# Modulation product of an adaLN transformer block, with its operands exchanged

## What is computed

```
def modulate(x, shift, scale):
    return rms_norm(x) * (1.0 + scale) + shift
def adaln(cond, w, b):
    return jnp.split(jax.nn.silu(cond) @ w + b, 6, axis=-1)
```

## Time and profile before

| | |
|---|---|
| median of 3 runs | 3432.3 us |
| the profiled execution | 3440.02 us |
| its span, first to last instruction | 3438.2 us |
| TensorE (PE) busy | 3122.3 us, 91% |
| TensorE weight loads (PEld) busy | 2324.8 us, 68% |
| VectorE (DVE) busy | 1697.6 us, 49% |
| ScalarE (ACT) busy | 963.3 us, 28% |
| mean granted TensorE clock | 0.941 of 2.4 GHz |

### The profile page before, as it was taken

One profiled execution on the slowest core, in us unless ns is written; L12 is line 12 of the kernel. 1 busy time (PEld: TensorE's weight loads), 2 busy tenths in 40 slices (PEclk: granted clock), 3 DMA queues, 4 the chain that ended last, 5 costly groups with the idle time before them and its releaser, 6 DMA issues. The chain is left out here.

```text
span 3438.2 us, 54550 instructions
## 1 busy us (share of the span) xinstructions
PE 3122.3 (91%) x24312; PEld 2324.8 (68%) x24312; DVE 1697.6 (49%) x2689; ACT 963.3 (28%) x1489; POOL 282.4 (8%) x362
## 2 busy tenths in 40 slices
PE   7999988799996977989978989999899999998899
PEld 2443333398994536888866979874579898455697
DVE  1104356465556108777755555455445453465453
ACT  1012310133331115443312333322223332142332
POOL 1202011000000012232310000000000000200000
PEclk9998989899998988999979999999999999999999
DMA  8311344245453210000024545542245554323253
GB/s 252 102 55 62 135 147 172 73 147 196 172 196 95 92 25 2 3 3 3 4 81 141 193 150 172 187 165 89 98 144 168 165 183 169 128 74 123 74 192 128
DMA packets 249827, 409.23 MB, mean 119 GB/s; under 512 B 10055, under 2 KB 102616, under 8 KB 249464
## 3 DMA queue, kind: packets, MB, share of 16 engines
q1 hardware_dynamic: 244824, 390.39, 33.3%
q0 software_dynamic: 4768, 15.35, 1.8%
HBM read 400.67 MB, written 2.95 MB: 117 GB/s over the span
## 5 line engine op out<-in xcount | busy, mean ns | idle before, releaser
L343 DVE TENSOR_TENSOR ring_parts<-ring,arena_parts 128x2048 fp32r<-128x2048 f32 x250 | 553.0, 2254 | 276.9 <-ACT arena_parts L336 274.6
L336 ACT CAST arena_parts<-ring 128x2048 fp32r<-128x2048 f32 x250 | 457.3, 1879 | 601.3 <-PE psum L2249 229.5
L2249 PE MATMUL psum<-arena_parts 128*128 128x256 f32 x2816 | 514.8, 286 | 6.4 <-DVE arena_parts L452 6.2
L2249 PEld LDWEIGHTS psum<-arena_parts 128*128 128x128 f32 x2816 | 444.0, 194 | 9.2 <-DVE arena_parts L452 9.2
L557 PE MATMUL psum<-ring,hT 128*128 128x512 f32 (+1 forms) x960 | 414.2, 593 | 9.1 <-DVE hT L1308 2.6
L2249 PE MATMUL psum<-arena_parts,ring_parts 128*128 128x256 f32 x1408 | 400.8, 285 | 0.0
L557 PEld LDWEIGHTS psum<-ring,hT 128*128 128x128 f32 x960 | 184.0, 192 | 234.5 <-issue 223.1
L380 PE MATMUL psum<-arena_parts 128*128 128x512 f32 x928 | 291.9, 396 | 8.3 <-DVE arena_parts L2285 8.1
L2249 PEld LDWEIGHTS psum<-arena_parts,ring_parts 128*128 128x128 f32 x1408 | 272.9, 194 | 0.0
L1381 PE MATMUL psum<-arena_parts 128*128 128x512 f32 x768 | 240.5, 395 | 7.8 <-DVE arena_parts L1428 7.8
L380 PEld LDWEIGHTS psum<-arena_parts 128*128 128x128 f32 x928 | 176.8, 191 | 46.6 <-DVE arena_parts L2285 9.0
(11 more groups left out here) (407 smaller groups left out, 5095.4 us busy)
## 6 DMA issues: line engine op xcount, KB each, us to landing
ring<-in_mlp_w SPq DMA_DIRECT2D x48, 2048.0 KB, 7.8
ring<-in_ada_w SPq DMA_DIRECT2D x24, 2048.0 KB, 8.0
ring<-in_ffn_pre_w_gu SPq DMA_DIRECT2D x44, 1024.0 KB, 6.9
ring<-in_ffn_post_w_gu SPq DMA_DIRECT2D x44, 1024.0 KB, 7.1
ring<-in_ffn_pre_w_down SPq DMA_DIRECT2D x8, 2048.0 KB, 7.9
ring<-in_xmem_wkv SPq DMA_DIRECT2D x8, 2048.0 KB, 8.1
ring<-in_ffn_post_w_down SPq DMA_DIRECT2D x8, 2048.0 KB, 7.8
ring<-in_ab_w_in SPq DMA_DIRECT2D x7, 2048.0 KB, 8.3
```

The source lines that it names most:

```text
L336: nc.scalar.copy(high_view(name)[:, k, :], raw_view(name)[:, k, :]).then_inc(*up(act, ("high", name, h)))
L343: nc.vector.tensor_tensor(low_view(name)[:, k, :], raw_view(name)[:, k, :], high_view(name).bitcast(F32)[:, k, :], ALU.subtract)\
L2249: ins = nc.tensor.matmul(psum[:, b, 256 * j:256 * j + 256], s[:, k, at:at + P], x_parts[q][:, k, :], start=(k == 0 and i == 0), stop=(k == ...
```

## The change

The product is computed the other way round. A block of 128 x 128 of the weights is now the stationary operand, and `sil`, the two condition columns (128 x 2 for each k), is the moving one. A slab is 4 blocks of columns (j) by 8 of rows (k): 32 matmuls in place of 8. The result stands in PSUM as columns, two for each j. `ada_matmuls` yields after each j, so a slab is 4 steps, and the fills are halved in number: 1 step per attention unit and per place in `ml_pe`, 12 steps in place of 24 before `decay_pe`.

The bias is loaded once, transposed into `colC` in the setup, and added by VectorE while it copies the columns from PSUM into `modcol`. The rows (wanted only in DRAM, for the gates) are made afterwards from `modcol`, by one or two transposes for parts 1 and 2, a copy by ScalarE and stores in rows of 128. Part 0 has no rows. The store of part 2 moves behind the gate loads on GpSimd.

```
+        sil = area(23136, KT, 2)
+        colC = adab[:, 0:96]
...
+            nc.sync.dma_start(sc2[0:96, 0, 0:P], a["ada_b"].rearrange("l (r p) -> (l r) p", p=P))\
+                .then_inc(landing("ada_b"), 16)
...
-            nc.gpsimd.memset(csil, 0.0).then_inc(*up(pool, "csil zero"))
-            pool.wait_ge(*latest(pool))
...
-            for part, (layer, n0, ns, base) in enumerate(ADA_PARTS):
-                for v in range(2):
-                    nc.gpsimd.dma_start(adab[base + v:base + 2 * ns:2, :],
...
+            pe.wait_ge(*when(("dma", "ada_b")))
+            pe.wait_ge(*bank(2, ("vec", 2)))
+            nc.tensor.transpose(psum[:, 2, 0:96], sc2[0:96, 0, 0:P], ident[0:96, 0:96]).then_inc(*up(pe, ("vec", "turned", 2)))
...
-            nc.tensor.matmul(rows, ident[at, at], adab[at, :], start=True, stop=False)
             for i in range(ns):
                 name = (f"ada{layer}", n0 + i, 0)
-                for k in range(KT):
+                for j in range(4):
                     stage(pe, "ada")
                     s = slab(pe, name)
-                    ins = nc.tensor.matmul(rows, csil[:, k, 22 - 2 * i:22 - 2 * i + 2 * ns], s[:, k, :],
-                                           start=False, stop=(i == ns - 1 and k == KT - 1))
-                    if k == KT - 1:
+                    at = 8 * i + 2 * j
+                    for k in range(KT):
+                        ins = nc.tensor.matmul(psum[:, b, at:at + 2], s[:, k, P * j:P * j + P], sil[:, k, :],
+                                               start=(k == 0), stop=(k == KT - 1))
+                    if j == 3:
...
+        def ada_cols_dve(dve, part):
+            dve.wait_ge(*when(("ada", "full", part)))
+            src = psum[:, ADA_BANK[part], 0:8 * ns].rearrange("p (c v) -> p v c", v=2)
             for v in range(2):
                 at = 48 * v + 4 * n0
+                nc.vector.tensor_tensor(modcol[:, layer, at:at + 4 * ns], src[:, v],
+                                        colC[:, 48 * layer + 4 * n0:48 * layer + 4 * n0 + 4 * ns], ALU.add)\
...
+        def ada_turn_pe(pe, part, b):
+            pe.wait_ge(*when(("mod", part)))
+            pe.wait_ge(*bank(b, ("mod", part)))
+            for v in range(ADA_ROWS[part][1]):
+                at = 48 * v + 4 * n0
+                ins = nc.tensor.transpose(psum[0:4 * ns, b, P * v:P * v + P], modcol[:, layer, at:at + 4 * ns], ident)
...
+        def ada_rows_act(act, part, b):
+            act.wait_ge(*when(("mod", "turned", part)))
+            nc.scalar.copy(adab[0:4 * ns, at:at + P * nv], psum[0:4 * ns, b, 0:P * nv])\
...
@@ ml_pe, at two places
-                fill(pe, queue, 2)
+                fill(pe, queue, 1)
...
@@ TensorE
-            fill(pe, ada[0], 16)
             first_turn_pe(pe, "L0a")
             fill(pe, ada[0], 8)
             first_turn_pe(pe, "C0a")
-            fill(pe, ada[0], 8)
-            fill(pe, ada[0], 1)
-            ada_turn_pe(pe, 0, 3)
+            fill(pe, ada[0], 9)
             ab_in_pe(pe)
...
-            att_pe(pe, "na", na, [("read", ("qkT", i)) for i in range(8)], ada[1], 2)
-            att_pe(pe, "cx", cxa, (), ada[1], 2)
+            att_pe(pe, "na", na, [("read", ("qkT", i)) for i in range(8)], ada[1], 1)
+            att_pe(pe, "cx", cxa, (), ada[1], 1)
             fill(pe, ada[1], 1)
-            fill(pe, ada[2], 24)
+            fill(pe, ada[2], 12)
+            ada_turn_pe(pe, 1, 7)
...
-            ada_turn_pe(pe, 1, 2)
             ada_turn_pe(pe, 2, 3)
@@ ScalarE
             att_act(act, "cx", cxa, 0.125)
-            ada_rows_act(act, 1)
             softplus_act(act)
+            ada_rows_act(act, 1, 7)
             decay_act(act)
             mlT_act(act)
             ml_act(act)
-            ada_rows_act(act, 2)
             act.wait_ge(*when(("read", ("merge", 3))))
+            ada_rows_act(act, 2, 3)
@@ VectorE
+            ada_cols_dve(dve, 1)
             decay_dve(dve)
...
             merge_dve(dve)
-            ada_turn_dve(dve, 1, 2)
-            ada_turn_dve(dve, 2, 3)
+            ada_cols_dve(dve, 2)
@@ GpSimd
             ml_pool(pool)
-            ada_store_pool(pool, 2)
             merge_pool(pool)
             pool.wait_ge(*when(("dma", "mod 1")))
-            pool.wait_ge(*when(("dma", "mod 2")))
...
+            ada_store_pool(pool, 2)
+            pool.wait_ge(*when(("dma", "mod 2")))
             norm_pool(pool, "L0m")
```

More of the change, by code:

```diff
@@ L571, in bidir_dual_stack @@
         HB = 12288
-        csil = area(23136, KT, 46)
+        sil = area(23136, KT, 2)
+        colC = adab[:, 0:96]
         pad = arena[0:56, 23000:23127]
@@ L596, in setup_pool @@
                 .then_inc(landing("ctx"), 16)
-            for part, (layer, n0, ns, base) in enumerate(ADA_PARTS):
-                for v in range(2):
-                    nc.gpsimd.dma_start(adab[base + v:base + 2 * ns:2, :],
-                                        a["ada_b"][layer, 512 * n0:512 * (n0 + ns)].rearrange("(i f) -> i f", f=512))\
-                        .then_inc(landing(f"ada_b {part}"), 16)
             nc.gpsimd.memset(half[:, :], -0.5).then_inc(*up(pool))
@@ L652, in setup_dve @@
                 dve.wait_ge(*latest(dve))
+            dve.wait_ge(*when(("vec", "turned", 2)))
+            nc.vector.tensor_copy(colC, psum[:, 2, 0:96]).then_inc(*up(dve, ("read", ("vec", 2))))
+            dve.wait_ge(*latest(dve))
         def setup_act(act):
             act.wait_ge(*when(("read", ("vec", 1))))
-            act.wait_ge(*when("csil zero"))
             for i, name in enumerate(("c", "c_ctx")):
-                nc.scalar.activation(csil[:, :, 22 + i], colB[:, ROWS_B[name]:ROWS_B[name] + 8], ACT.Silu).then_inc(*up(act, "silu c"))
+                nc.scalar.activation(sil[:, :, i], colB[:, ROWS_B[name]:ROWS_B[name] + 8], ACT.Silu).then_inc(*up(act, "silu c"))
@@ L659, in setup_act @@
                 act.wait_ge(*latest(act))
-        ADA_PARTS = ((0, 0, 4, 64), (0, 4, 8, 32), (1, 0, 12, 0))
+        ADA_PARTS = ((0, 0, 4), (0, 4, 8), (1, 0, 12))
         ADA_BANK = (2, 6, 0)
+        ADA_ROWS = (None, (96, 2), (352, 1))
         def ada_matmuls(pe, part):
-            layer, n0, ns, base = ADA_PARTS[part]
-            rows = psum[0:2 * ns, ADA_BANK[part], :]
+            layer, n0, ns = ADA_PARTS[part]
+            b = ADA_BANK[part]
             stage(pe, "ada")
-            pe.wait_ge(*bank(ADA_BANK[part], ("ada", part)))
+            pe.wait_ge(*bank(b, ("ada", part)))
@@ L670, in ada_matmuls @@
             pe.wait_ge(*when("silu c"))
-            pe.wait_ge(*when(("dma", f"ada_b {part}")))
-            pe.wait_ge(*when(("dma", "const")))
-            at = slice(base, base + 2 * ns)
-            nc.tensor.matmul(rows, ident[at, at], adab[at, :], start=True, stop=False)
             for i in range(ns):
                 name = (f"ada{layer}", n0 + i, 0)
-                for k in range(KT):
+                for j in range(4):
                     stage(pe, "ada")
                     s = slab(pe, name)
-                    ins = nc.tensor.matmul(rows, csil[:, k, 22 - 2 * i:22 - 2 * i + 2 * ns], s[:, k, :],
-                                           start=False, stop=(i == ns - 1 and k == KT - 1))
-                    if k == KT - 1:
+                    at = 8 * i + 2 * j
[3 more added lines that the diff above has]
+                    if j == 3:
@@ L692, in fill @@
             stage(pe, held)
[L694 to L700, removed]
+        def ada_cols_dve(dve, part):
+            stage(dve, "ada")
+            layer, n0, ns = ADA_PARTS[part]
+            dve.wait_ge(*when(("ada", "full", part)))
+            src = psum[:, ADA_BANK[part], 0:8 * ns].rearrange("p (c v) -> p v c", v=2)
+            for v in range(2):
+                at = 48 * v + 4 * n0
+                nc.vector.tensor_tensor(modcol[:, layer, at:at + 4 * ns], src[:, v],
+                                        colC[:, 48 * layer + 4 * n0:48 * layer + 4 * n0 + 4 * ns], ALU.add)\
+                    .then_inc(*up(dve, ("read", ("ada", part)) if v else None))
+            also(("mod", part), ("read", ("ada", part)))
+            dve.wait_ge(*latest(dve))
@@ L702, in ada_turn_pe @@
         def ada_turn_pe(pe, part, b):
             stage(pe, "ada")
-            layer, n0, ns, base = ADA_PARTS[part]
-            at = slice(base, base + 2 * ns)
-            pe.wait_ge(*when(("ada", "rows", part)))
+            layer, n0, ns = ADA_PARTS[part]
+            pe.wait_ge(*when(("mod", part)))
             pe.wait_ge(*bank(b, ("mod", part)))
-            for j in range(4):
-                ins = nc.tensor.transpose(psum[:, b, 2 * ns * j:2 * ns * j + 2 * ns], adab[at, P * j:P * j + P], ident[at, at])
+            for v in range(ADA_ROWS[part][1]):
+                at = 48 * v + 4 * n0
+                ins = nc.tensor.transpose(psum[0:4 * ns, b, P * v:P * v + P], modcol[:, layer, at:at + 4 * ns], ident)
@@ L710, in ada_turn_pe @@
             ins.then_inc(*up(pe, ("mod", "turned", part)))
```

(16 more changed lines are left out.)

## The result

The change makes the kernel slower: 3636.9 us median (3634.6 to 3641.2, 4 runs) against 3431.5 us (4 runs), a ratio of 1.060, 95% interval 1.058 to 1.062. The forecast was 3650 us.

A forecast was written before the change was run, and what follows sets the result against it. TensorE, busy 91%, was taken as the bound, its clock deciding. Terms +23 start, -1.9 bias, +98 attentions, +19 fill, +79 mLSTM, +1.4 waits give +218: 3658 us profiled, median 3650; own bounds 3600 to 3680, full range 3500 to 3680.

The forecast's parts named there:

- the clock decides: Every stretch where the two-column product is a large part: TensorE stays at 1.2 GHz, a slab taking 13.65 us, twice 6.93.
- Rival A: Every stretch of the product: full weight loads keep the high clock, so not slower, 3430 us; chance 18%.
- C: Rival, whole product: loads take 0.11 us at either clock level and only the rest slows, +80, 3512 us; chance 4%.
- B: Rival: clock low only where the product stands alone or with thin work, attentions rising as now, +120, 3552 us; chance 6%.
- The high clock's "no change": Modulation product at 2.4 GHz: a turned-round slab takes 7.0 us against 6.93, so 24 slabs cost +2 us.
- the 64-column row: Profile row of products with 128 x 128 stationary and 64 moving columns, records 0.110 us apart, used to price a slab.
- Attentions and fill together: Attentions +98 us, units about 8.4 us low against 4.48 high; fill of three slabs +19 us, 41.0 against 21.8.
- mLSTM, +79: mLSTM stretch at the low clock: steps 1.85 times the high ones, 206 us with waits in place of 125.6.
- the new fill 5.0 low: mLSTM step: 5.12 us at the low clock today, taken as 5.0 us with the changed product's fill.
- Start, +23: Kernel start up to `ab_in`: four slabs and context transposes at the low clock +24.9 us, less 1.1 and 1.
- the wide transposes: Context's transposes in the start, which may bring some microseconds of high clock: -1 us.
- Waits, +1.4: TensorE waits: about 0.8 us more at `decay_act`, 0.6 us between merge and `ab_out`; bounds 0 and 3.

## Why the prediction was right

**Direction and cause.** The step "the clock decides" held: at 1.2 GHz a record starts every 0.213 us whether its load has 4 rows or 128, at 2.4 GHz every 0.110 to 0.112 with the same loads, and in no stretch that the two-column product filled alone did the level rise. Rival A (loads hold it) is refuted by the changed kernel's own trace, C by the 0.213, B by attentions at 0.51, where I had given it 6%. The experiment with 128 columns, which changes nothing but the number of columns moved, shows that this number is the cause.

**The high clock's "no change".** Forecast 7.0 us a slab from the 64-column row; with 128 columns moving it is 64 x 0.112 = 7.2 us, against 6.93 for the old product. So the exchange alone gains nothing even at 2.4 GHz: 8192 columns are loaded for a slab now, and 8192 were moved before.

**Terms of the sum.** Attentions and fill together were right to 3 us (+111.8 for +115; a unit 8.46 us, forecast 8.4, the fill 41.2, forecast 41.0). Three were mis-sized:
- mLSTM, +79 forecast, +67 measured. The step that failed is "the new fill 5.0 low": I took the old low step of 5.12 us and changed only the fill. The timeline of the changed kernel shows 4.71:

```profile
610.08 0.80 PE L1207 MATMUL psum<-arena,sc 128*128 128x129 f32 x2 [2.79 <-DVE sc L1254]
...
611.53 3.41 PE L680 MATMUL psum<-arena,ring 128*128 128x2 f32 x16
614.80 0.78 PE L1207 MATMUL psum<-arena,sc 128*128 128x129 f32 x2
...
619.51 0.78 PE L1207 MATMUL psum<-arena,sc 128*128 128x129 f32 x2
```

From the fill's start to the next product it is 614.80 - 611.53 = 3.27 us, not the 3.41 of 16 records by themselves, and the three products before it take 1.45 us in place of the 1.6 that 5.0 leaves for them. 0.3 us times 32 steps is 9 of the 12 us.
- Start, +23 forecast, +19.8 measured. I had given the wide transposes 1 us of regained clock; they regained 3.0 (24.3 us for the second two slabs in place of 27.3). And the chain from the last product to `ab_in` shortened from 3.3 us to 1.5, by 1.8 and not 1.1, as VectorE's adds follow the product directly:

```profile
72.60 0.26 DVE L702 TENSOR_TENSOR modcol<-psum,adab 128x16 f32<-128x16 f32 x2 [53.54 <-PE psum L680]
72.89 0.24 DVE L524 TENSOR_SCALAR stat<-modcol 128x8 f32<-128x8 f32 x2
```

- Waits, +1.4 forecast. At `decay_act` the idle time of TensorE grew from 4.4 us to 5.05, as forecast (ScalarE's copy of 0.36 us and the transposes stand ahead of it):

```profile
583.36 0.36 ACT L724 COPY adab<-psum 32x256 f32<-32x256 f32 x1 [41.03 <-PE psum L716]
583.74 1.28 ACT L1104 ACT_TABLE_LOAD   x1
...
588.32 3.58 PE L1119 MATMUL psum<-const,arena 4*128 4x4 f32 x32 [5.05 <-ACT arena L1108]
```

 Beyond it the transposes ahead of the mLSTM ran longer at 0.50 (a mean of 0.59 over 7.3 us), which I had not priced. Before `ab_out` the added step is there (VectorE's adds at 813.26, a transpose at 813.63, `ab_out` at 813.83), but the stage as a whole is 0.9 shorter.

**Behind `ab_out`** the span is 6.6 us shorter with the same code. I had taken nothing for that. It is within the spread of this part: in the ten profiled executions it took 2819.0 to 2828.0 us, and the changed kernel's is the shortest.

**Where luck came in.** Up to `ab_out` the sum said +218 and the two profiled executions differ by 201.3: the forecast was 17 us too high there, 12 of them the mLSTM, 3 the start and 3 the attentions, while the gates, the merge and the stretch after `ab_in` nearly cancel. Yet the medians of four runs each, 3431.5 and 3636.9, differ by 205.4. The profiled execution of before stands 8.6 us above its median and that of after (3634.6) 2.3 below, so that 3650 is too high by only 13. That the number came so close is in part due to which executions were profiled, and not to the terms of the sum.

## What to carry to other kernels

Exchanging the operands of a product with few columns trades moved columns for loaded ones. In this float32 kernel with blocks of 128 x 128 that was no better than even at the high clock (7.0 to 7.2 us a slab against 6.9), and with two columns moving the engine stayed at half its clock, which made the other matmuls of the stage slower too (an attention unit 8.46 us against 4.48): 138 us of the product's own and some 63 of its neighbours'. Before such a change look in the trace for the nearest stream with few moving columns, and at the granted clock beside it, not at the busy share. If the orientation is wanted for another reason (results as columns, a shorter chain), try repeating the moving columns: with 128 a slab took 7.2 us here, against 6.9 for the old product, and 210 us came back, while with 64 only 68 did. Product steps placed where the engine waited shortened the kernel by another 20 us; how much of that is the filled idle time and how much the clock was not told apart.

## What was not expected of the hardware

- With the same loads, 2, 32, 64 and 128 moving columns gave 3637, 3597, 3569 and 3427 us: two thirds of the gain came with the last step. At 64 columns TensorE did nothing but this product for 43 us at 0.50, and for 14.4 us at 0.99 where it had entered at the high level.
- In the changed kernel the level was back behind 3.4 us of transposes that move 128 columns, and the two-column product behind them had it for only about 4 us: 48 to 52 us has a mean of 0.95, 52 to 60 has 0.50.

```profile
48.00:52.00 4.00, 4.00 (x36) 0.95 1.05 401
52.00:60.00 8.00, 8.00 (x39) 0.50 0.03 8
```

- Records with a load of 128 columns are 0.112 us apart at 2.4 GHz with 128 columns moving, 0.110 with 64 and 0.111 with 2 (36 in the 4 us above): up to 128 the moving columns are nearly free.
